# Scaling over 128 partitions, and the sliding attention's unit in the middle of each block's steps

## The reference, cut to what matters

```python
# A: forgetting attention, 8 heads of 64, causal, in blocks of queries
logits = einsum('bqhd,bkhd->bhqk', q, k) * scale + F[q] - F[k]
ya = (softmax(where(causal, logits, -1e30)) @ v) * silu(za)
# B: sliding window, 8 query heads on 2 kv heads, chunks of 64, window 128, with a sink
logits = einsum('bcqhgd,bcshd->bchgqs', qc, kb) * scale - slope * dist
yb = (softmax(concat([logits, sink]))[..., :128] @ vb) * silu(zb)
merged = sigmoid(ga) * (ya @ w_o_fox) + sigmoid(gb) * (yb @ w_o_swa)
```

## Time and profile before

| | us |
|---|---|
| median of 3 runs | 2205.91 (2197.71 to 2218.35) |
| profiled execution | 2219.62 |
| its span | 2217.9, mean granted clock 0.939 |
| attend, from the first step's last matmul | 1147.85 to 1818.40 |
| PE's first matmul of the merge | 1840.51 |

### The profile page before, as it was taken

How to read it: one execution, slowest core, us unless ns; L and a number is a source line. 1 busy time by engine, 2 the same in 40 slices (tenths; PEclk the granted TensorE clock), 3 DMA queues, 4 the chain that set the end, 5 groups by cost and what they waited for, 6 DMA issues and landing times. The chain is left out here.

```text
span 2217.9 us, 28286 instructions
## 1 busy us (share of the span) xinstructions
PE 2037.9 (92%) x9722; PEld 1615.4 (73%) x9722; DVE 980.5 (44%) x1915; ACT 755.8 (34%) x1439; POOL 568.6 (26%) x534
## 2 busy tenths in 40 slices
PE   7489999999999999999869989989989977998998
PEld 2367878788788788888746666666666747998887
DVE  1945555652221400000054556577566645564332
ACT  1622222220121412212137666667666662101100
POOL 0610000000000000000017556566576562120000
PEclk9589999999999999999959889899998988999999
DMA  6233343444321212211172643534534315232222
GB/s 228 95 98 105 104 123 94 135 141 105 119 86 47 64 68 85 85 47 66 57 159 63 140 104 75 130 89 105 127 92 107 83 28 191 85 124 95 95 99 81
DMA packets 230057, 222.98 MB, mean 101 GB/s; under 512 B 53618, under 2 KB 187634, under 8 KB 227380
## 3 DMA queue, kind: packets, MB, share of 16 engines
q1 hardware_dynamic: 218180, 181.74, 29.5%
q0 software_dynamic: 11648, 39.85, 5.7%
q10 hardware_dynamic: 128, 0.13, 0.0%
HBM read 149.58 MB, written 72.09 MB: 100 GB/s over the span
## 5 line engine op out<-in xcount | busy, mean ns | idle before, releaser
L1017 POOL TENSOR_TENSOR Pl<-PT,Ph 128x512 fp32r<-128x512 f32 (+2 forms) x382 | 431.5, 1146 | 278.7 <-ACT Ph L1152 261.4
L454 PE MATMUL pj<-hTh,Wh 128*128 128x512 f32 x768 | 299.5, 390 | 0.6 <-DVE Wl L646 0.2
L455 PE MATMUL pj<-hTl,Wh 128*128 128x512 f32 x768 | 298.8, 389 | 0.0
L456 PE MATMUL pj<-hTh,Wl 128*128 128x512 f32 x768 | 298.8, 389 | 0.0
L454 PE MATMUL pj<-Wh,hTh 128*128 128x512 f32 (+1 forms) x640 | 246.3, 385 | 23.7 <-DVE Wl L646 23.6
L365 POOL DMA_DIRECT2D wraw<-in_w_in x84 | 45.1, 537 | 857.1 <-DVE Wl L646 851.2
L1145 ACT ACTIVATE PT<-sc 128x512 f32<-128x512 f32 (+2 forms) x382 | 199.0, 521 | 162.8 <-PE sc L1073 60.3
L455 PE MATMUL pj<-Wl,hTh 128*128 128x512 f32 (+1 forms) x640 | 240.2, 375 | 0.0
L456 PE MATMUL pj<-Wh,hTl 128*128 128x512 f32 (+1 forms) x640 | 240.1, 375 | 0.0
L1233 DVE TENSOR_REDUCE part_max<-mx 128x1 f32<-128x512 f32 (+3 forms) x288 | 169.0, 598 | 115.1 <-PE mx L1042 114.3
L1152 ACT ACTIVATE Ph<-PT 128x512 fp32r<-128x512 f32 (+2 forms) x382 | 214.3, 561 | 12.1
(11 more groups left out here) (214 smaller groups left out, 3647.7 us busy)
## 6 DMA issues: line engine op xcount, KB each, us to landing
qk_scratch<-qThl SPq DMA_DIRECT2D x96, 256.0 KB, 2.8
wraw<-in_w_in POOLq DMA_DIRECT2D x88, 256.0 KB, 3.9
g_scratch<-st SPq DMA_DIRECT2D x64, 256.0 KB, 2.4
gt<-g_scratch SPq DMA_DIRECT2D x16, 1024.0 KB, 7.8
xin<-in_x POOLq DMA_DIRECT2D x16, 512.0 KB, 4.7
wada<-in_w_ada SPq DMA_DIRECT2D x8, 1024.0 KB, 7.7
z_scratch<-st SPq DMA_DIRECT2D x32, 256.0 KB, 2.4
Qb<-qk_scratch SPq DMA_DIRECT2D x32, 256.0 KB
```

The lines of the kernel that those rows point to most:

```text
L454: nc.tensor.matmul(out, a_hi, b_hi, start=first, stop=False)
L455: nc.tensor.matmul(out, a_hi, b_lo, start=False, stop=False)
L456: return nc.tensor.matmul(out, a_lo, b_hi, start=False, stop=last)
L1017: pool.tensor_tensor(Pl[n % NPH][0:rows, 0:w], PT[n % NP][0:rows, 0:w], Ph[n % NPH][0:rows, 0:w].bitcast(F32), ALU.subtract).then_inc(low_ ...
```

## The change

It does these things:

- The steps of an s block stand after half of the f block's key tiles, no longer behind the block. The output bank follows the order in which blocks begin: (i + (kind == "s")) % 2, and the first gather of a block waits for that bank's last user (`before`).
- A batch is now made of two f blocks of each partition half and four s blocks, so that all 8 sums lie as 4 x 2 rows, and one L1285 of 128 partitions scales what were two f blocks (or the s blocks of a whole tile): 4 instructions a batch, three steps apart, 8 batches. R is always 4 x 512 over 128 partitions.
- The stationary operand of the value products is 65 columns wide (64 of V and one column of ones) and no longer 128; V's rows shrink from 192 to 132 elements, and there are 4 PT buffers instead of 3.
- The due times of V follow the moved steps.

```diff
     for i in range(NB):
+        keys = JB * (i % JB + 1)
         first["f", i] = len(steps)
-        steps += [("f", i, kb) for kb in range(JB * (i % JB + 1))]
-        last["f", i] = len(steps) - 1
+        steps += [("f", i, kb) for kb in range(keys // 2)]
         first["s", i] = len(steps)
         steps += [("s", i, part) for part in (("A", "B") if i >= 2 else ("A",))]
         last["s", i] = len(steps) - 1
+        steps += [("f", i, kb) for kb in range(keys // 2, keys)]
+        last["f", i] = len(steps) - 1
+    step_no = {step: n for n, step in enumerate(steps)}
...
+    out_bank = lambda kind, i: (i + (kind == "s")) % 2
+    before, user = {}, {}
+    for b in sorted(first, key=lambda b: first[b]):
+        before[b] = user.get(out_bank(*b))
+        user[out_bank(*b)] = b
...
-    NSC, NMX, NP, NPH = 3, 3, 3, 4
+    NSC, NMX, NP, NPH = 3, 3, 4, 4
+    VW, OUT = 2 * HD + 4, HD + 1
...
-    batches, e0 = [], 0
-    for size in [8] * 7 + [6, 2]:
-        batches.append((e0, size))
-        e0 += size
+    place = lambda kind, i: (i // 8 * 2 + i % JB // 2, i % JB % 2) if kind == "f" else (i // 4, 2 + i // 2 % 2)
+    members = [[e for e, b in enumerate(blocks) if place(*b)[0] == k] for k in range(8)]
     turns, free = [], START
-    for e, size in batches:
-        turns.append(max(last[blocks[e + size - 1]] + 5, free))
-        free = turns[-1] + 13 + size
+    for units in members:
+        turns.append(max(last[blocks[units[-1]]] + 5, free))
+        free = turns[-1] + 24
...
-    scale_at = when(((k, e), n + 13 + m) for k, n in enumerate(turns) for m, e in enumerate(range(batches[k][0], sum(batches[k]))))
-    TAIL = 22
+    scale_at = when(((k, m), n + 13 + 3 * m) for k, n in enumerate(turns) for m in range(4))
+    TAIL = 28
...
-                if opening and e >= 2:
-                    pe.wait_ge(y_done, e - 1)
-                    pe.wait_ge(sum_copied, e - 1)
+                if opening and before[kind, i]:
+                    pe.wait_ge(y_done, number[before[kind, i]] + 1)
+                    pe.wait_ge(sum_copied, number[before[kind, i]] + 1)
...
-                nc.tensor.matmul(part(slice(0, P)), values[:, HD:3 * HD], high, start=opening and kind == "f", stop=False)
+                nc.tensor.matmul(part(slice(0, OUT)), values[:, HD:HD + OUT], high, start=opening and kind == "f", stop=False)
...
-            def scale(k, e):
-                half, m = e % 2, (e - batches[k][0]) // 2
+            def scale(k, m):
                 dve.wait_ge(r_in, 48 * (k + 1))
-                dve.wait_ge(y_done, e + 1)
-                for out, r in zip(out_of(e), parts_of(e, R[half * HD:(half + 1) * HD, m, :])):
-                    last_op = nc.vector.tensor_tensor(out, out, r, ALU.mult)
-                last_op.then_inc(scaled, 1)
+                dve.wait_ge(y_done, members[k][-1] + 1)
+                if m < 2:
+                    j = k % 2 * 2 + m
+                    y, r = yT[:, k // 2, j * QW:(j + 1) * QW], R[:, m, :]
+                else:
+                    t = 2 * k + m - 2
+                    y, r = yT[:, 4:8, t * P:(t + 1) * P], R[:, m, :].rearrange("p (a n) -> p a n", n=P)
+                nc.vector.tensor_tensor(y, y, r, ALU.mult).then_inc(scaled, 1)
```

More of the change, by code:

```diff
@@ L819, in attend @@
     q_due = when((i, START + 2 * i if i < NQ else last["f", i - NQ] - AHEAD + 1) for i in range(NB))
-    v_due = when(((h, c), START + 3 + 2 * c if not h else last["f", h * JB - 1] - 15 + 4 * c + 4) for h in range(FOX_H) for c in range(JB))
+    v_due = when(((h, c), START + 3 + 2 * c if not h else step_no["f", h * JB - 1, 4 * c + 3] + 1) for h in range(FOX_H) for c in range(JB))
     s_due = when((t, START + 1 + 7 * t if t < 2 else last["s", 2 * t - 3] + 1) for t in range(TT))
@@ L853, in attend @@
         KBa, KBb = ([sb(f"{n}{k}", [P, KV_H, WIN], F32R) for k in range(2)] for n in ("KBa", "KBb"))
-        VA = [sb(f"VA{k}", [P, KV_H, 3 * HD], F32R) for k in range(2)]
-        VB = [sb(f"VB{k}", [HD, KV_H, 3 * HD], F32R) for k in range(2)]
+        VA = [sb(f"VA{k}", [P, KV_H, VW], F32R) for k in range(2)]
+        VB = [sb(f"VB{k}", [HD, KV_H, VW], F32R) for k in range(2)]
         identr, maskr = sb("identr", [P, P], F32R), sb("maskr", [P, P], F32R)
@@ L907, in load_v @@
                 if h:
-                    sp.wait_ge(pv_done, last["f", h * JB - 1] - 15 + 4 * c + 4)
+                    sp.wait_ge(pv_done, step_no["f", h * JB - 1, 4 * c + 3] + 1)
                 rows = slice(c * QW, (c + 1) * QW)
@@ L1110, in gather @@
                     if opening:
-                        nc.tensor.matmul(part(slice(0, P)), pick, QBa[t % 2][0:HD + 4, g * GH:(g + 1) * GH, :], start=True, stop=False)
+                        nc.tensor.matmul(part(slice(0, OUT)), pick, QBa[t % 2][0:HD + 4, g * GH:(g + 1) * GH, :], start=True, stop=False)
                 pe.wait_ge(cast_done, n + 1)
-                nc.tensor.matmul(part(slice(0, P)), values[:, HD:3 * HD], high, start=opening and kind == "f", stop=False)
+                nc.tensor.matmul(part(slice(0, OUT)), values[:, HD:HD + OUT], high, start=opening and kind == "f", stop=False)
                 nc.tensor.matmul(part(slice(0, HD)), values[:, 0:HD], high, start=False, stop=False)
                 pe.wait_ge(low_done, n + 1)
-                nc.tensor.matmul(part(slice(0, P)), values[:, HD:3 * HD], low, start=False, stop=closing).then_inc(pv_done, 1)
+                nc.tensor.matmul(part(slice(0, OUT)), values[:, HD:HD + OUT], low, start=False, stop=closing).then_inc(pv_done, 1)
             for n in range(START, NS):
@@ L1165, in copy_sums @@
                     act.wait_ge(sum_out[e % NZ], 16 * (e // NZ))
-                nc.scalar.activation(sums[e % NZ], bank_o[e % 2][HD:HD + 1, :], ACT.Copy).then_inc(sum_copied, 1)
+                nc.scalar.activation(sums[e % NZ], bank_o[out_bank(*blocks[e])][HD:HD + 1, :], ACT.Copy).then_inc(sum_copied, 1)
                 act.wait_ge(sum_copied, e + 1)
-                act.dma_start(dram["sums"][e:e + 1], sums[e % NZ]).then_inc(sum_out[e % NZ], 16)
+                kind, i = blocks[e]
+                k, m = place(kind, i)
+                if kind == "f":
+                    act.dma_start(dram["sums"][k, m, i // JB % 2:i // JB % 2 + 1], sums[e % NZ]).then_inc(sum_out[e % NZ], 16)
+                else:
+                    act.dma_start(dram["sums"][k, m, :, i % 2 * 2 * P:(i % 2 + 1) * 2 * P].rearrange("s (a n) -> a s n", n=P),
+                                  sums[e % NZ].rearrange("o (a s n) -> o a s n", s=2, n=P)).then_inc(sum_out[e % NZ], 16)
             for n in range(START, NS + 1):
@@ L1270, in collect @@
                 dve.wait_ge(pv_done, last[blocks[e]] + 1)
-                for out, y, z in zip(out_of(e), parts_of(e, bank_o[e % 2][0:HD, :]), parts_of(e, Z[e % NZ][0:HD, :])):
+                for out, y, z in zip(out_of(e), parts_of(e, bank_o[out_bank(*blocks[e])][0:HD, :]), parts_of(e, Z[e % NZ][0:HD, :])):
                     last_op = nc.vector.tensor_tensor(out, y, z, ALU.mult)
@@ L1296, in _ @@
                     invert(k)
-                for k, e in scale_at(n):
-                    scale(k, e)
+                for k, m in scale_at(n):
+                    scale(k, m)
 def split_rows(nc, ctx, tag, sources, ring, Wh, Wl, early=()):
@@ L1564, in build @@
         "shift_b": scratch("shift_b", [TT, 2 * SWA_H, 2, P]),
[L1565 to L1566 removed]
+        "sums": scratch("sums", [FOX_H, 4, 2, COLS]),
+        "inv": scratch("inv", [FOX_H, 4, 2, COLS]),
         "gate": scratch("gate_scratch", [1, D]),
```

37 lines of the change are left out of this document (16 added, 21 removed).

## The result

The changed kernel took 2227.28 us (median of 8 runs, 2220.55 to 2254.81), the kernel before 2206.39 (8 runs, 2197.71 to 2218.35): ratio **1.0089 [1.0057, 1.0121]**, some 20 us slower. I forecast 2199, faster by 7, with "faster by over 1%" as the likeliest of the three outcomes. The time lies inside the range, the sign is wrong. The profiled execution of after took 2225.47 us, near its median; that of before 13 above its own. So the two traces differ by 5.8 us only, and understate the loss.

What follows compares the result with a forecast made beforehand. Nothing is saturated for a whole head; waits and half-clock stretches at heads' starts and the scaling cost time. Terms -24.5 - 34.7 + 51 - 2 + 3 = -7 give 2199 us, range 2140 to 2232 (forecast's own 2179 to 2217).

Steps and rivals of the forecast that it cites:

- Scaling, -24.5: Steps 16 to 33 of the heads: 32 wide scalings replace 96, shrinking DVE's backlog; net 24.5 us faster.
- Rival 3: Scalings at steps 33 to 42 make their own backlog in heads 1, 3 and 5: +22, 2221 us; chance 0.05.
- Mid-head wait, +51: Step 19: row load late behind load_s, in heads 2, 4 and 6 also behind R; 51 us slower.
- Heads' start, -34.7: Steps 1 to 7: earlier row load regains 39.5 us, less 4.8 for late queries; 34.7 us faster.
- rival 2: Heads' starts: queries over 1.5 us late for step 1's first maximum, clock falls; +42, 2241 us; chance 0.18.
- The rest, -2: One more PT buffer eases ACT's waits for POOL: 2 us faster (0 to 8); 65 stationary columns count zero.
- Tail, +3: From the last attention matmul to the merge: larger R and wider scalings, 3 us slower (0 to 6).
- The sum: All terms over the whole kernel: 7 us faster, 2199 us; chance 0.42.

## Why the prediction was wrong

- **Scaling, -24.5**: right. By the ratios the exchange is -24 (-22 by the medians), with the longer tail in it; I had -24.5 + 3. With the unit behind its block, steps 16 to 33 gained 30.0; I had 34.9 less three times 0.8, 32.5. The 2.5 us a head for scalings on steps 33 to 42 did not come: steps 34 to 48 went from 146.1 to 143.3 there. Rival 3 is dead.
- **Mid-head wait, +51**: right in mechanism and size. I had 45 of it in heads 1 to 6. In the kernel with the unit behind its block steps 16 to 48 took 307.7 us, after 354.0, with equally many matmuls: 46.3. (In steps 16 to 33 alone it is 208.37 - 164.41 = 44.0, with the 36 moved matmuls in it.) The row load was 7 to 8 us late in heads 2, 4 and 6 (forecast 8), about 2.1 in the odd ones (forecast 1.7). The range of the forecast, 2179 to 2217, does not follow from the bounds that I gave for this term: 0 to 8 five times and 0 to 15 three times make 2148 to 2233. Of the two halves of the Trainium skill's rule on rings (DMA: Bandwidth & Descriptors, Queues, rings and completion order), the first, descriptors consumed in ring order, agrees with the 17.0 us from load_s to PE's score, and with the wait that fell from 29.7 to 13.0 us as R went behind. No run here shows the second.
- **Heads' start, -34.7**: this is the step that failed. I wrote: "leaving about 6.6 us, for Ka and Q (900 KB) behind the V chunk and load_s's rest: 6.5 to 7.5. I take 0.8 us in each of six heads (bounds 0 and 2) and a clock that holds, since head 4 held it with 1.5". In head 3 it left 5.3 and took 9.0. My own numbers spoke against it: load_s at step -8 and K at -3 lie five steps apart, 6.8 us at the 9.5 that I gave to seven (6.6 in the trace of after, 1390.02 to 1396.63), and I had load_s hold the queue for 9.4, so that it could not have cleared, as I argued against rival 2. The waits were 1.2 to 3.7 us, 13.4 in all for my 4.8. The clock then fell to 0.63, 0.59 and 0.56 in heads 2, 3 and 5. Gained were 6.7 us instead of 34.7, **28 too few**. Putting the queries first took 9.8 of the 13.4 us away, brought 149.0 us in the trace and 0.9867 for 1.0089 in the runs, so the queries' place in the queue is shown as the cause. The 39.5 us at the heads' starts could be had, but not by this placement: with the unit at the block's end and the first row early, steps 1 to 7 took 60.59 us, 10.1 a head.
- **Rival 2** is what happened, at two thirds of its price (28 of 42 us): its place (the first maximum on Q, step 1) and the fallen clock hold, its point of decision (1.5 us late in each head) doesn't. Head 6 held clock 1.00 with a 2.1 us wait, head 2 lost it with 1.7. One head at 1.5 us was no ground for "a clock that holds".
- **The rest, -2**: mis-sized. These two edits alone gave 0.56%, about 12 us (6 to 19 by the interval), where I had bounds of 0 and -8. In the traces most of it lies in steps 1 to 7 (100.86 to 84.96), where the clock held in more heads; why it held stays open.
- **Tail, +3**: the time from the last attention matmul to the merge went from 22.1 to 23.7 us, +1.6, with R as forecast (7.4 for 7.7).
- **The sum.** The traces of before and after differ by +5.8 us where I had -7, a miss of 13. The 28 us of the heads' starts were offset there by luck: head 7 gained 5 us (67.8 to 62.8) where I had a loss of 3.5, and steps 16 to 48 lost 13.5 where I had 20. The rest of the miss, up to the +20 of the runs, is the 13 us by which the profiled execution of before stood above its median, and 2 by which that of after stood below; a sum over one trace cannot assign them to a step.

## What to carry to other kernels

Moving a unit of work moves its loads past everything else in the same queue. Write that queue's order before and after, with each transfer's hold time, and check every consumer's slack by subtraction, also that of work that wasn't moved. Then plan the small late load ahead of the large ones: four steps of lead were worth 3% here, against 2.6% that the placement had cost. A lead that cures one unit can starve the next (31.2 us on VB), so give it only to the unit whose load is late. And compare windows that hold the same work: equal steps did not, once planned maxima had moved.

## What the runs showed of the hardware

- A short wait can cost more than itself: where 9.8 us of waiting at the heads' starts went, 27.3 us went in all, with steps behind a wait at a mean granted clock of 0.56 to 0.63. That is one trace of each kernel; the same kernel profiled twice had a head's start at 14.34 us and clock 0.94, and at 19.53 and 0.56. But the same 2 us wait was followed by clock 1.00 in head 6 of after and 0.56 in head 3 with the queries first. No length of wait separates the two in these runs.
- A DVE multiplication of 128x512 took 1137 ns on average beside POOL (28 of them), less than the 1423 ns of a 64x256 before, with four times the elements.
- Shrinking a matmul's stationary side from 128 to 65 columns, together with one more buffer, was worth about half a per cent (0.9944), more than I had read out of the waits in the trace of before. The two were not separated.
